# Five small tables moved between the large on-chip buffers of a two-model transformer kernel

## Chip, core and metric

One core of a Trainium2 chip runs the whole program in one launch. The metric is the time of one execution on the device in microseconds (us). Its engines are TensorE (PE: matmuls; its weight loads are listed apart as PEld), VectorE (DVE), ScalarE (ACT), GpSimd (POOL) and SyncE (SP, which here only issues transfers).

## What is computed

256 tokens of width 1024 pass through two blocks, each of two layers, all in float32. Cut to its large products:

```python
for l in range(2):                                   # first block
    mod = silu(c) @ ada_w[l] + ada_b[l]              # nine shifts, scales and gates
    hn = modulate(rms_norm(h)); h = h + 0.5*g1 * ((silu(hn @ gate) * (hn @ up)) @ w_out)     # ffn1, width 2816
    hn = modulate(rms_norm(h)); z = hn @ w_in[l]     # 2564 columns: diff attention, conv, gMLP, forgetting attention
    h = h + g2 * (mixed @ w_out[l])
    hn = modulate(rms_norm(h)); h = h + 0.5*g3 * swiglu(hn)                                  # ffn2, width 2816
for l in range(2):                                   # second block
    proj = rmsnorm(x) @ w_in_2[l]                    # 7680 columns: q, k, v of 24 heads, and gates
    x = x + (gates * three attention outputs) @ w_o
    x = x + square(relu(rmsnorm(x) @ w_up)) @ w_down # width 4096
```

## The kernel before

**Weights in parts.** The large products aren't done in plain float32. Each float32 weight chunk is split into a rounded high part and a rest: SP loads 1 MB chunks (128 partitions x 8 k-tiles x 256 columns) into the four slots of `ring`; ACT writes the high part (`round_half`, L1187: `w_hi <- ring`); POOL writes the low part (`split`, L682: `w_lo = ring - w_hi`), both in halves of a chunk, and `w_hi` and `w_lo` have two slots each. The activations are split too: `hn`/`hn_lo` hold the normed input (8 k-tiles x 256 tokens), and the hidden layers lie in `gated` and `up2`, two views of the one large buffer `arena`. A product of a k-tile and 128 output columns is then three matmuls of 256 moving columns in fp32r, issued by `terms` (L716 in the trace):

```python
for i, (a, b) in enumerate(((w, x), (w, x_lo), (w_lo, x))):
    if token_major:
        a, b = b, a
    last = mm(out, a, b, start=start and i == 0, stop=stop and i == 2)
```

The first of `a, b` is the stationary operand, which a weight load (PEld) brings in, 128 columns of 4 bytes (512 bytes a partition); the second streams, 256 columns of 4 bytes (1024 bytes a partition). A weight chunk of 8 k-tiles and 256 columns is 8 x 2 x 3 = 48 matmuls. `product` reads `hn` and `hn_lo` (phases f1in, z, f2in, z2, up) and `out_product` reads `gated` or `up2` (f1out, f2out, dn). In v-type units of z and z2 (`token_major`) hn and hn_lo are the stationary operands and the weights' parts stream. The first unit of a phase, whose k-tiles come in one after another, has lines of its own (L747, L748, L751). The products `o`, `y` and `wo` (L800, L1124) are plain float32 straight from `ring` with moving operands in `arena`.

**Order of the work.** Each engine's program is written out by hand and synchronised by counting semaphores. `fill` on SP waits until POOL is done with the ring slot. While f1in and f2in run, SP also loads 2 MB chunks of `ada_w` into `arena` (`ada_fill`), one after every pair of weight chunks, for DVE to reduce (L1558). Attention heads (L929, L963, L964, L707) are interleaved with units of z2 in the second block.

**Where buffers begin.** The buffers in a partition are laid one behind the other in the order of their declarations; each begins at a multiple of 32 bytes. A slice that a matmul reads begins a multiple of 512 bytes behind its buffer's start, for `w_hi`, `w_lo`, `hn`, `hn_lo`, `gated` and `up2` alike, so the distance of two operands modulo 512 bytes is that of their buffers. Before, all from `w_hi` to `const` have sizes that are multiples of 512 bytes and so begin at distance 0; `const` has 3959 columns, and behind it come `mod` (288 bytes), `der` (256), `cond` (32), `norm2` (160), `stat` (256), `small` (256), `ident_r` and `unseen` (512 each), then `arena`.

Of the kernel before, what the change touches and what calls it, by code (L numbers as in the profile page):

```python
# [19 lines left out]
F32R = mybir.dt.float32r  # L20
# [6 lines left out]
S = 256  # L27
L = 2
KT = D // P
# [5 lines left out]
MOD_TILES = 9 * KT  # L35
# [353 lines left out]
def build(nc, dram, out, at, old):  # L389

    plan = Plan()
    with ExitStack() as ctx:
        def sb(name, *shape, dtype=F32):
            return ctx.enter_context(nc.sbuf_tensor(name, [P, *shape], dtype))
# [5 lines left out]
        ring = sb("ring", RING, 8, 256)  # L400
        w_hi, w_lo = sb("w_hi", 2, 8, 256, dtype=F32R), sb("w_lo", 2, 8, 256, dtype=F32R)
        h = sb("h", KT, S)
        hn, hn_lo = sb("hn", KT, S, dtype=F32R), sb("hn_lo", KT, S, dtype=F32R)
        square, square_sum = sb("square", 2, S), sb("square_sum", S)
        rstd = sb("rstd", S)
        n_const = dram["constants"].shape[1]
        const = sb("const", n_const)
        mod = sb("mod", MOD_TILES)
        der = sb("der", 64)
        cond = sb("cond", KT)  # L410
        norm2 = sb("norm2", 40)
        stat = sb("stat", 4, 16)
        small = sb("small", 64)
        ident_r, unseen = sb("ident_r", P, dtype=F32R), sb("unseen", P, dtype=F32R)
        arena = sb("arena", ARENA)
        arena_at = nc.sbuf_base - 4 * ARENA

# [1644 lines left out]
```

## Time and profile before

| | |
|---|---|
| median of 3 runs | 2059.44 us (2059.37 to 2059.82) |
| the profiled execution's own time | 2062.2 us |
| its span | 2060.4 us, 36118 instructions |
| mean granted TensorE clock | 0.981 of full speed |
| PE busy | 1981.9 us (96%), 15210 matmuls |
| PEld busy | 1905.0 us (92%) |
| POOL busy | 1320.9 us (64%) |
| ACT busy, DVE busy | 939.7 us (46%), 826.5 us (40%) |
| moved by DMA | 398.21 MB, mean 193 GB/s |

The span runs from the first to the last instruction; the own time of an execution is 1.8 us more. Matmuls are pipelined, so that a record's length (its mean ns) is longer than the distance from its start to the next one's; how fast PE goes is seen by counting matmuls in a stretch. Idle time of an engine that nobody waits for costs nothing.

### The profile page before, as it was taken

What the parts mean: (1) busy time and instruction counts of PE and PEld (TensorE: products, weight loads), DVE (VectorE), ACT (ScalarE), POOL (GpSimd) and SP (SyncE); (2) the same over time, 40 slices, a digit from 0 to 9 for tenths busy, and PEclk for the clock granted to TensorE, in tenths of its full rate; (3) what the DMA queues carried; (4) which work ended last, traced back from release to release, by engine and by line L of the source; (5) the groups of instructions that cost most, each with busy time, mean ns of one, the idle gap of its engine ahead of it and who ended that gap; (6) DMA issues with size and microseconds to landing.
All of it is one profiled execution on the core that took longest, in us unless ns stands there. A gap on an engine that the chain in (4) does not pass through costs nothing.

```text
span 2060.4 us, 36118 instructions
## 1 busy us (share of the span) xinstructions
PE 1981.9 (96%) x15210; PEld 1905.0 (92%) x15210; DVE 826.5 (40%) x1747; ACT 939.7 (46%) x1467; POOL 1320.9 (64%) x612
## 2 busy tenths in 40 slices
PE   6999997999999999889999999999999999999998
PEld 3999996899999998779999999989999999989998
DVE  3674576372147466735113522133302522133311
ACT  2444554344454445434445354534544354525543
POOL 0888760388878887217887865506897955506895
PEclk8999998999999999999999999999999999999999
DMA  9998650695599786127545643346564643335562
GB/s 319 361 341 294 215 158 21 212 360 167 182 306 364 267 261 190 65 80 259 190 159 174 203 143 113 114 128 193 184 200 136 222 144 103 123 123 185 184 205 82
DMA packets 356786, 398.21 MB, mean 193 GB/s; under 512 B 8984, under 2 KB 318992, under 8 KB 356624
## 3 DMA queue, kind: packets, MB, share of 16 engines
q1 hardware_dynamic: 356464, 395.70, 58.5%
q8 instruction: 120, 1.97, 0.4%
q14 instruction: 42, 0.34, 0.1%
q10 hardware_dynamic: 160, 0.20, 0.0%
HBM read 394.82 MB, written 1.05 MB: 192 GB/s over the span
## 4 chain that ended last, share of the span: by engine, by line
PE 88%; DVE 4%; ACT 3%; POOL 1%; issue 1%; SPq 1%; DMA 1%; DVEq 0%; ACTq 0%
PE bank L716 70%; PE bank L800 6%; PE bank L1124 3%; POOL w_lo L682 1%; PE bank L963 1%; PE bank L929 1%; SPq L544 1%; DVE arena L1701 1%; DVE bank L1630 1%; ACT arena L1323 1%; PE bank L707 1%; PE bank L751 1%; PE bank L747 1%; ACT w_hi L1187 1%; PE bank L1025 1%
## 5 line engine op out<-in xcount | busy, mean ns | idle before, releaser
L682 POOL TENSOR_TENSOR w_lo<-ring,w_hi 128x1024 fp32r<-128x1024 f32 (+2 forms) x608 | 1320.7, 2198 | 720.0 <-ACT w_hi L1187 719.8
L716 PE MATMUL bank<-hn,w_hi 128*128 128x256 f32 x2752 | 786.3, 286 | 3.3 <-POOL w_lo L682 2.9
L716 PE MATMUL bank<-hn_lo,w_hi 128*128 128x256 f32 x2752 | 778.6, 283 | 0.0
L716 PE MATMUL bank<-hn,w_lo 128*128 128x256 f32 x2752 | 778.6, 283 | 0.0
L1187 ACT ACTIVATE w_hi<-ring 128x1024 fp32r<-128x1024 f32 (+2 forms) x608 | 578.6, 976 | 416.2 <-PE bank L716 381.1
L716 PEld LDWEIGHTS bank<-hn,w_hi 128*128 128x128 f32 x2752 | 527.9, 192 | 7.1 <-POOL w_lo L682 5.3
L716 PEld LDWEIGHTS bank<-hn_lo,w_hi 128*128 128x128 f32 x2752 | 528.0, 192 | 1.1 <-issue 0.5
L716 PEld LDWEIGHTS bank<-hn,w_lo 128*128 128x128 f32 x2752 | 527.9, 192 | 0.0
L716 PE MATMUL bank<-gated,w_hi 128*128 128x256 f32 x1408 | 239.6, 276 | 0.0
L716 PEld LDWEIGHTS bank<-gated,w_hi 128*128 128x128 f32 x1408 | 212.0, 188 | 0.0
L716 PE MATMUL bank<-gated,w_lo 128*128 128x256 f32 x704 | 194.3, 276 | 0.0
L716 PE MATMUL bank<-up,w_hi 128*128 128x256 f32 x1024 | 174.2, 276 | 0.0
L1558 DVE SCALAR_TENSOR_TENSOR bank<-arena,cond,bank 128x512 f32<-128x512 f32 x204 | 154.2, 756 | 7.3
L716 PEld LDWEIGHTS bank<-up,w_hi 128*128 128x128 f32 x1024 | 154.1, 188 | 0.0
L716 PE MATMUL bank<-up,w_lo 128*128 128x256 f32 x512 | 141.3, 276 | 0.0
L716 PEld LDWEIGHTS bank<-gated,w_lo 128*128 128x128 f32 x704 | 132.1, 188 | 0.0
L800 PE MATMUL bank<-arena,ring 128*128 128x256 f32 x512 | 116.1, 390 | 5.1 <-DVE arena L1994 3.2
L800 PEld LDWEIGHTS bank<-arena,ring 128*128 128x128 f32 x512 | 100.1, 196 | 20.7 <-DVE arena L1994 4.0
L1658 DVE TENSOR_TENSOR bank<-arena,bank 128x512 f32<-128x512 f32 x44 | 30.6, 696 | 219.5 <-PE bank L716 219.5
L1275 ACT ACTIVATE arena<-bank 128x512 f32<-128x512 f32 x44 | 26.3, 598 | 172.8 <-PE bank L716 172.2
L1323 ACT ACTIVATE arena<-arena,stat 128x128 f32<-128x128 f32 x120 | 53.2, 444 | 102.7 <-DVE stat L1715 44.0
L716 PEld LDWEIGHTS bank<-up,w_lo 128*128 128x128 f32 x512 | 96.1, 188 | 0.0
(203 smaller groups left out, 2222.4 us busy)
## 6 DMA issues: line engine op xcount, KB each, us to landing
ring<-in_ffn_w_in SPq DMA_DIRECT2D x88, 1024.0 KB, 6.7
ring<-in_w_in SPq DMA_DIRECT2D x72, 1024.0 KB, 5.1
arena<-in_ada_w SPq DMA_DIRECT2D x35, 2048.0 KB, 10.2
ring<-in_w_up SPq DMA_DIRECT2D x32, 1024.0 KB, 5.5
ring<-in_w_down SPq DMA_DIRECT2D x32, 1024.0 KB, 5.1
ring<-in_ffn_w_out SPq DMA_DIRECT2D x32, 768.0 KB, 4.7
ring<-in_ffn_w_out SPq DMA_DIRECT2D x32, 640.0 KB, 4.1
ring<-in_w_in SPq DMA_DIRECT2D x16, 512.0 KB, 3.7
```

The costliest lines, as they stand in the source:

```text
L544: sp.dma_start(dst, src).then_inc(rows_in, 16)
L682: pool.tensor_tensor(w_lo[:, q, ks], ring[:, r, k0:k0 + n], w_hi[:, q, ks], ALU.subtract) \
L707: i = pe.transpose(dst, src, ident[0:n, 0:n])
L716: last = mm(out, a, b, start=start and i == 0, stop=stop and i == 2)
L747: mm(outs[c], w_hi[:, q, kw, ws], hn[:, kx], start=kx == 0 and c == 0, stop=False)
L800: last = mm(outs[c], ring[:, s, k, c * P:(c + 1) * P], x[:, k0 + k, :], start=(k0 + k == 0), stop=(k0 + k == total - 1))
L1124: last = mm(b[:, c], ring[:, s, k0 + k, c * P:(c + 1) * P], o2[:, k0 + k, :], start=(k == 0), stop=(k == nk - 1))
L1187: f(w_hi[:, q, half * 4:half * 4 + n], ring[:, r, k0:k0 + n], ACT.Copy).then_inc(weights_rounded, 1)
L1275: f(act_tmp[:, j], bank[:, 2 * j], ACT.Silu).then_inc(silu_done, eng.step(f"{s} silu {p}", silu_done))
L1323: f(t, t, ACT.Exp, bias=st[:, b + j:b + j + 1], scale=scale, accum_out=st[:, 10 + 2 * m + j:11 + 2 * m + j]) \
L1558: stt(part, src[:, k], col(cond, k), part, ALU.mult, ALU.add).then_inc(vector_done, eng.step())
L1658: tt(bank[:, 2 * j], act_tmp[:, j], bank[:, 2 * j + 1], ALU.mult) \
```

## The change

Only declarations move. `der` is laid before `hn`; `mod`, `cond` and a new unused `spare` of 16 columns lie between `hn` and `hn_lo`; a new unused `more` of 24 columns lies before `arena`. No instruction is added, removed or put elsewhere in any engine's order, and all sizes, slices and waits stay; line numbers behind the place grow by one (L716 becomes L717).

```diff
         h = sb("h", KT, S)
-        hn, hn_lo = sb("hn", KT, S, dtype=F32R), sb("hn_lo", KT, S, dtype=F32R)
+        der = sb("der", 64)
+        hn = sb("hn", KT, S, dtype=F32R)
+        mod, cond, spare = sb("mod", MOD_TILES), sb("cond", KT), sb("spare", 16)
+        hn_lo = sb("hn_lo", KT, S, dtype=F32R)
         square, square_sum = sb("square", 2, S), sb("square_sum", S)
         rstd = sb("rstd", S)
         n_const = dram["constants"].shape[1]
         const = sb("const", n_const)
-        mod = sb("mod", MOD_TILES)
-        der = sb("der", 64)
-        cond = sb("cond", KT)
         norm2 = sb("norm2", 40)
         stat = sb("stat", 4, 16)
         small = sb("small", 64)
         ident_r, unseen = sb("ident_r", P, dtype=F32R), sb("unseen", P, dtype=F32R)
+        more = sb("more", 24)
         arena = sb("arena", ARENA)
```

Added up, the buffers begin at these distances from `w_hi`, modulo 512 bytes:

| buffer | before | after |
|---|---|---|
| ring, w_lo, h | 0 | 0 |
| hn | 0 | 256 |
| hn_lo | 0 | 128 |
| square, square_sum, rstd, const | 0 | 128 |
| arena (so gated, up2 and the attention's views) | 192 | 352 |

Distances within `arena` stay as they were, and so does the distance of `ring` to the weights' parts.

## Rows read from the trace of the kernel before

**Rows 1.** The page: span, busy time, and the chain that ended last, by line

```profile
span 2060.4 us, 36118 instructions
PE 1981.9 (96%) x15210; PEld 1905.0 (92%) x15210; DVE 826.5 (40%) x1747; ACT 939.7 (46%) x1467; POOL 1320.9 (64%) x612
PE 88%; DVE 4%; ACT 3%; POOL 1%; issue 1%; SPq 1%; DMA 1%; DVEq 0%; ACTq 0%
```

**Rows 2.** PE's groups by form: count, busy us, mean ns, idle before and its releaser

```profile
L716 PE MATMUL bank<-hn,w_hi 128*128 128x256 f32 x2752 | 786.3, 286 | 3.3 <-POOL w_lo L682 2.9
L716 PE MATMUL bank<-hn_lo,w_hi 128*128 128x256 f32 x2752 | 778.6, 283 | 0.0
L716 PE MATMUL bank<-hn,w_lo 128*128 128x256 f32 x2752 | 778.6, 283 | 0.0
L716 PE MATMUL bank<-gated,w_hi 128*128 128x256 f32 x1408 | 239.6, 276 | 0.0
L716 PE MATMUL bank<-gated,w_lo 128*128 128x256 f32 x704 | 194.3, 276 | 0.0
L716 PE MATMUL bank<-up,w_hi 128*128 128x256 f32 x1024 | 174.2, 276 | 0.0
L716 PE MATMUL bank<-up,w_lo 128*128 128x256 f32 x512 | 141.3, 276 | 0.0
...
L716 PE MATMUL bank<-w_lo,hn 128*128 128x256 f32 x288 | 81.4, 283 | 0.0
...
L747 PE MATMUL bank<-hn,w_hi 128*128 128x256 f32 x160 | 46.5, 309 | 15.3 <-ACT hn L1247 11.0 <-ACT hn L1245 4.2
```

**Rows 3.** The chain in 950:1000, products of hn: start us, us, matmuls

```profile
949.95 50.16 PE bank L716 x418
```

**Rows 4.** The chain in 1500:1550, products of up2

```profile
1500.00 50.09 PE bank L716 x442
```

**Rows 5.** Windows of 50 us: PE, PEld, DVE, ACT, POOL, clock, DMA share, GB/s

```profile
950.00:1000.00 50.00, 50.00 (x419) 50.00 (x418) 14.41 (x21) 21.93 (x26) 41.94 (x18) 1.00 0.54 172
1500.00:1550.00 50.00, 50.00 (x443) 50.00 (x443) 2.99 (x7) 20.68 (x23) 46.42 (x20) 1.00 0.61 197
1900.00:1950.00 50.00, 50.00 (x419) 50.00 (x419) 17.56 (x26) 24.95 (x35) 42.02 (x18) 1.00 0.61 190
```

**Rows 6.** Timeline of PE from 269.75, token-major units: start us, us

```profile
269.75 0.28 PE L716 MATMUL bank<-w_hi,hn 128*128 128x256 f32 x1
269.87 0.28 PE L716 MATMUL bank<-w_hi,hn_lo 128*128 128x256 f32 x1
269.99 0.28 PE L716 MATMUL bank<-w_lo,hn 128*128 128x256 f32 x1
```

**Rows 7.** PE in 1346:1371, plain float32 with ring and arena

```profile
L1124 PE MATMUL bank<-arena,ring 128*128 128x256 f32 x117 | 25.4, 379 | 0.0
```

**Rows 8.** POOL's groups by form, whole span

```profile
L682 POOL TENSOR_TENSOR w_lo<-ring,w_hi 128x1024 fp32r<-128x1024 f32 x448 | 1064.3, 2401 | 646.3 <-ACT w_hi L1187 646.1
```

**Rows 9.** Windows over the stages that also load ada_w, columns as in Rows 5

```profile
60.00:160.00 100.00, 100.00 (x836) 100.00 (x835) 71.50 (x98) 43.13 (x51) 83.88 (x36) 1.00 1.06 350
...
600.00:670.00 70.00, 70.00 (x585) 70.00 (x585) 52.89 (x73) 31.47 (x38) 57.91 (x26) 1.00 1.06 360
```

**Rows 10.** Timeline of ACT from 148.98, idle before and its releaser in brackets

```profile
149.48 2.00 ACT L1187 ACTIVATE w_hi<-ring 128x1024 fp32r<-128x1024 f32 x2
151.97 1.06 ACT L1187 ACTIVATE w_hi<-ring 128x1024 fp32r<-128x1024 f32 x1 [0.50 <-DMA ring<-in_ffn_w_in]
```

**Rows 11.** The chain in the second block's attention, from 1208.62

```profile
1208.62 0.67 PE bank L929 x4
1209.46 0.29 DVE arena L1701
...
1211.07 2.44 DVE arena L1745 x6
...
1214.82 1.54 ACT arena L1323 x7
1216.57 0.68 ACT arena L1323 x3
1217.25 3.79 ACT w_hi L1187 x4
...
1251.76 5.76 PE bank L716 x48
```

## The prediction

> **What bounds the kernel now.** I read the page first. PE is busy for 96% of the span and the chain that ended last is PE for 88% of it [rows 1]; what makes matmuls quicker is worth its full size, and little else is. The groups by form come next, because they keep operands apart [rows 2]. All fp32r products have the same shape, 128x128 stationary and 256 moving columns, and yet the records of those with hn and hn_lo last 283 to 286 ns, and those with gated and up (the view up2) 276 ns. Records overlap, so this doesn't give the rate. The rate is read from the chain in a stretch with nothing but such matmuls: 418 matmuls with hn in 50.16 us, 120.0 ns each [rows 3], against 442 with up in 50.09 us, 113.3 ns each [rows 4]. In both stretches PE and PEld are busy throughout and the granted clock is 1.00 (2.4 GHz) [rows 5]: no wait and no clock accounts for the 6.7 ns.
>
> Is it what the other engines do meanwhile? The windows say no [rows 5]: with DVE busy 14.41 us of 50 or 17.56 us, the count with hn is 419 both times; in the faster stretch POOL is busier (46.42 us against 41.94), and so is the DMA (197 GB/s against 172). The token-major units, where hn is the stationary operand and w_hi and w_lo stream, start every 0.12 us as well [rows 6]. So it lies in the pair of buffers, whichever side streams. Two things set the pairs apart: hn and hn_lo begin 0 bytes from w_hi and w_lo modulo 512, gated and up2 192 bytes; and hn lies near the weights' parts (within some 57 KB) while arena lies far off. The change alters the first and hardly the second.
>
> **The change, part by part.** No instruction is added, removed or moved, so the sum has only rates in it.
>
> *hn 0 to 256 bytes, hn_lo 0 to 128.* L716 has 3 x 2752 matmuls on them [rows 2] and 3 x 288 more in token-major form (one of its three rows stands there): 9120. L747, L748 and L751 add 3 x 160 = 480 [rows 2], which I leave out: they wait for the norm's k-tiles (15.3 us before L747) and run partly at the lower clock. No row shows distances of 256 and 128. The bounds: from above, 120.0 ns as now (nothing excludes a loss, but no fp32r row is slower at full clock); from below, the quickest streaming that the trace shows. Plain float32 takes 25.4 us for 117 records of 256 columns [rows 7], 217 ns each. As 256 columns at 2.4 GHz, one a cycle, are 106.7 ns, I count such a record as two passes, and half of it, 108.5 ns, is my estimate for a stream that meets no hindrance. I take 113.3 ns, the only measured value of the same instruction at a distance other than 0: 9120 x 6.67 ns = 60.8 us.
>
> *arena 192 to 352 bytes.* 2112 matmuls with gated and 1536 with up [rows 2], 3648 in all. Now 113.3 ns; bounds again 108.5 and 120.0 ns, thus -17.5 us to +24.4 us. Both distances are off 0, so I take no change.
>
> *const, square, mod, der, cond.* Their matmuls are few and their ACT and DVE work has 50% and more idle time; nothing.
>
> *What is not passed on.* Three covers get thinner. (a) POOL: a chunk costs it 2 x 2.40 us = 4.80 us [rows 8] and PE 48 x 0.1200 = 5.76 us now, 5.44 us at 113.3 ns, 5.21 us at 108.5 ns. PE stays the slower one; 0. (b) The ring's loads while ada_w is loaded too: a pair of chunks and one ada chunk are 4 x 1.049 MB = 4.19 MB. In 11.52 us that is 364 GB/s, in 10.88 us 385 GB/s; the windows show 350 to 360 GB/s at a DMA share of 1.06 [rows 9], which is full. In the first f1in the ring already loses its lead: at 151.97 ACT waits 0.50 us for the ring's transfer [rows 10]. There some 16 chunks x 48 x 6.67 ns = 5.1 us of PE's gain runs into the data's arrival; ACT and POOL work about half a chunk ahead of PE, which takes back some 2 us, so 3 us are lost. In the later ones (600:670) ACT doesn't wait for a transfer, and I take nothing off. (c) In the second block's attention some stretches have DVE and ACT on the chain [rows 11], about 25 us a layer, with some 5 chunks of matmuls beside it: 2 x 5 x 48 x 6.67 ns = 3.2 us lost; where heads and 48-matmul units alternate on the chain (1251.76) the gain counts fully.
>
> Sum: 60.8 - 3 - 3.2 = 54.6 us. The profiled execution's own 2062.2 us becomes 2007.6 us; the runs shown have a median 2.8 us lower, so I forecast 2059.4 - 54.6 = 2004.8, say 2005 us.
>
> **A rule against it.** The rows show two rates for one instruction, 120.0 and 113.3 ns [rows 3, 4]. The Trainium skill, "SBUF — State Buffer", section "Who interferes with whom", gives PE two independent read ports, one for the moving operand and one for the weight load, and says that PE waits for nobody; by that the distance between the two operands can't matter, and the sum would be 0. It offers no reason for the 6.7 ns that the rows show, so I weigh it as what speaks for the no-change rival and not as the likeliest. Its page "TensorE: Matmul & The Clock Gate", section "Back-to-back issue gap", has 2.5 ns above the columns' time for a warm matmul, 109.2 ns here; every fp32r row of this trace is above it, and by it the sum for the whole would be 9120 x 10.8 + 3648 x 4.1 = 113 us, before covers.
>
> **The rivals.**
> - *Deeper gain.* 120.0 ns is 13.3 ns above the 106.7 ns in which 256 columns pass at 2.4 GHz, and 113.3 ns is 6.7 ns above: exactly half. If the weight load and the stream meet at some addresses, 192 bytes may be halfway and 128, 256 or 352 free. For it: room down to 108.5 ns. Against: no fp32r pair shows it. At the bound: 9120 x 11.5 + 17.5 us = 122 us, less some 8 us for (b) and (c), so 1945 us; with hn halfway to it, 1980 us.
> - *Only a part.* The repeating length may be 256 bytes, not 512: then hn at 256 is as bad as at 0, and only what pairs with hn_lo gets better, a third: 3040 x 6.67 = 20 us, 2039 us. For it: 192 and 0 differ modulo 256 as well.
> - *No change.* What matters is near or far (the same part of the memory), not the distance modulo 512. For it: each hn pair is near and each arena pair far, so the trace can't tell; the skill's two ports lean this way. Against: regular 120.0 ns for hn and hn_lo, w_hi and w_lo, though they lie at different distances in bytes. 2059 us.
> - *Slower.* Arena's new distance falls where the old one of hn was, while hn gains nothing: 3648 x 6.67 = +24 us, 2084 us; f1out, f2out and dn would be the places. It decides when hn gains less than 0.4 of what arena loses per matmul (3648/9120), i.e. under 2.7 ns against 6.7 ns.
>
> **How the numbers follow.** Forecast 0.46, deeper 0.22, a part 0.12, no change 0.12, slower 0.08. A measurement of this kernel can tell 0.2% (4 us) from nothing. Faster: 0.46 + 0.22 + 0.12 = 0.80; same 0.12; slower 0.08. The range has to keep 8 in 10: it takes in the first three, from 1945 us to 2045 us (20 us saved, and some of it lost). The likeliest case by itself is 1983 to 2020 us: 111 ns (9120 x 9.0 = 82 us) to 115 ns (9120 x 5.0 = 46 us), less the 6.2 us of covers.
>
> **What would show it.** The chain or count in a stretch of hn matmuls: 441 in 50 us instead of 418, records about 276 ns instead of 283. In stretches with up and gated still 441 to 443; any other count is arena's distance. If hn's three kinds get different spacings, the length that repeats is shorter than 512. The first f1in should show ACT waiting several us for ring<-in_ffn_w_in, against 0.5 us at 151.97. POOL's share in hn stretches should rise to about 44 us of 50. Wrong would be: 120 ns for hn still (then it is the region), or POOL's subtraction taking longer at the new addresses, since it has only 0.64 us a chunk to spare at 113.3 ns. All of it is read in stages, not in the sum: plain float32 (L1124, L800) should stay at 217 ns.

## The result, and the profile after

The changed kernel takes 2065.49 us (median of 16 runs) against 2060.28 us for the kernel before (16 runs): ratio 1.0023, 95% interval 1.0016 to 1.0030. It is 0.2% slower, where 2.6% faster (2005 us) was forecast, and it lies above the forecast range, which ended at 2045 us. The page of its profiled execution:

```profile
span 2064.3 us, 36118 instructions
PE 1985.2 (96%) x15210; PEld 1911.1 (93%) x15210; DVE 826.9 (40%) x1747; ACT 940.4 (46%) x1467; POOL 1319.5 (64%) x612
PE 88%; DVE 4%; ACT 3%; POOL 1%; issue 1%; SPq 1%; DMA 1%; DVEq 0%
L717 PE MATMUL bank<-hn,w_hi 128*128 128x256 f32 x2752 | 777.9, 283 | 2.1 <-POOL w_lo L683 1.8
L717 PE MATMUL bank<-hn,w_lo 128*128 128x256 f32 x2752 | 769.7, 280 | 0.0
L717 PE MATMUL bank<-gated,w_hi 128*128 128x256 f32 x1408 | 253.6, 283 | 0.0
L717 PE MATMUL bank<-up,w_hi 128*128 128x256 f32 x1024 | 184.4, 282 | 0.0
```

The page's totals hardly differ from those of before [rows 1]: same share of PE, same chain. The groups do differ, and in two directions: hn's records got a little shorter (283 and 280 ns for 286 and 283), those of gated and up longer (283 and 282 for 276) [rows 2]. The rates are in the chain of the same two stretches, 950:1000 for hn and 1500:1550 for up:

```profile
949.99 50.06 PE bank L717 x425
```

```profile
1500.00 50.04 PE bank L717 x417
```

With hn 50.06 us / 425 = 117.8 ns (it was 120.0 [rows 3]); with up 50.04 / 417 = 120.0 ns (it was 113.3 [rows 4]). The 864 token-major matmuls on hn gained less; in a stretch of them, 1648:1660, the chain has 119.2 ns each:

```profile
1647.93 12.16 PE bank L717 x102
```

Added up, 8256 x -2.2 ns and 864 x -0.8 ns are -19 us, and 3648 x +6.7 ns are +24 us, together +5 us. The medians differ by 5.2 us, the two profiled spans by 2064.3 - 2060.4 = 3.9 us. The change did act, by some 20 us on each side, and the sum hides it.

Nothing else moved by as much. POOL's subtraction takes what it took [rows 8], and in the first f1in ACT waits for the ring's transfer a little more than before (1.23 us where it was 0.50 [rows 10]); the rows of POOL by form and of ACT's timeline after:

```profile
L683 POOL TENSOR_TENSOR w_lo<-ring,w_hi 128x1024 fp32r<-128x1024 f32 x448 | 1062.2, 2396 | 638.6 <-ACT w_hi L1188 637.8
```

```profile
151.65 1.06 ACT L1188 ACTIVATE w_hi<-ring 128x1024 fp32r<-128x1024 f32 x1 [1.23 <-DMA ring<-in_ffn_w_in]
```

### The profile page after: what moved, and what is told of

The parts are those of the page before. It is cut to its first block, busy times and chain, and to the rows that moved or that the text cites. A ratio compares the mean times of both kernels' runs of the same rounds, so it can differ in the third digit from the quotient of the medians.

```text
span 2064.3 us, 36118 instructions
## 1 busy us (share of the span) xinstructions
PE 1985.2 (96%) x15210; PEld 1911.1 (93%) x15210; DVE 826.9 (40%) x1747; ACT 940.4 (46%) x1467; POOL 1319.5 (64%) x612
## 4 chain that ended last, share of the span: by engine, by line
PE 88%; DVE 4%; ACT 3%; POOL 1%; issue 1%; SPq 1%; DMA 1%; DVEq 0%
PE bank L717 71%; PE bank L801 6%; PE bank L1125 3%; POOL w_lo L683 1%; PE bank L964 1%; PE bank L930 1%; DVE arena L1702 1%; SPq L545 1%; DVE bank L1631 1%; ACT arena L1324 1%; PE bank L748 1%; PE bank L708 1%; ACT w_hi L1188 1%; PE bank L752 1%; PE bank L1026 1%
## 5 line engine op out<-in xcount | busy, mean ns | idle before, releaser
L717 PE MATMUL bank<-hn,w_hi 128*128 128x256 f32 x2752 | 777.9, 283 | 2.1 <-POOL w_lo L683 1.8
L717 PE MATMUL bank<-hn_lo,w_hi 128*128 128x256 f32 x2752 | 775.1, 282 | 0.0
L717 PE MATMUL bank<-hn,w_lo 128*128 128x256 f32 x2752 | 769.7, 280 | 0.0
L717 PEld LDWEIGHTS bank<-hn,w_hi 128*128 128x128 f32 x2752 | 517.8, 188 | 5.9 <-POOL w_lo L683 3.9
L717 PEld LDWEIGHTS bank<-hn,w_lo 128*128 128x128 f32 x2752 | 519.3, 189 | 0.0
L717 PEld LDWEIGHTS bank<-hn_lo,w_hi 128*128 128x128 f32 x2752 | 516.7, 188 | 1.0 <-issue 0.5
L717 PE MATMUL bank<-gated,w_hi 128*128 128x256 f32 x1408 | 253.6, 283 | 0.0
L717 PEld LDWEIGHTS bank<-gated,w_hi 128*128 128x128 f32 x1408 | 215.8, 187 | 0.0
L717 PE MATMUL bank<-gated,w_lo 128*128 128x256 f32 x704 | 197.3, 280 | 0.0
L717 PE MATMUL bank<-up,w_hi 128*128 128x256 f32 x1024 | 184.4, 282 | 0.0
L717 PEld LDWEIGHTS bank<-up,w_hi 128*128 128x128 f32 x1024 | 157.7, 188 | 0.0
L717 PE MATMUL bank<-up,w_lo 128*128 128x256 f32 x512 | 144.2, 282 | 0.0
L717 PEld LDWEIGHTS bank<-gated,w_lo 128*128 128x128 f32 x704 | 133.9, 190 | 0.0
L717 PEld LDWEIGHTS bank<-up,w_lo 128*128 128x128 f32 x512 | 96.6, 189 | 0.0
```

## Experiments

### A map of distances (e1_map)

The kernel's stages give one distance each. This program measures many: it fills one fp32r buffer from x and runs 46 streams of 96 matmuls with nothing else going on, each stream on a source line of its own. The distances go up in steps of 32 bytes, so that each stream stands behind the one with the next smaller distance.

```python
for a in run(0, 41152, 8192, 0): last = mm(a[0], a[1], a[2], start=a[3], stop=a[4])  # near 192
```

The arguments are where w_hi and x begin (bytes), how far behind x its low part is, and whether it is token-major.

> A measuring program, not the model: it fills one large fp32r buffer and then runs 46 streams of 96 matmuls with the shapes, slices and order of the products (w_hi,x; w_hi,x_lo; w_lo,x; eight k-tiles, two column halves, twice), one stream a source line, with x at a set distance from the weights, near (40960 bytes and the distance) or far (112128 bytes and the distance). Its output is not the model's. Distance theory: the time per matmul is a function of the distance of weights and x modulo 512 bytes alone. Then near and far give the same at each of the 16 distances, with 120.0 ns at 0, 113.3 ns at 192, 119.9 ns at 352, 117.8 ns for 256 with the low part at 128, and moving both operands by 64 bytes changes nothing. Place theory: what counts is whether the two operands lie near or far, or their own addresses. Then near stays at 118 to 120 ns at every distance and far 0 is at 113 ns, or moving both by 64 bytes changes the time.

The timeline of the map, start us and us of each stream, for near 0 (L78), near 192 (L84), near 256 (L86), far 0 (L94) and their followers:

```profile
62.86 11.68 PE L78 MATMUL bank<-buf 128*128 128x256 f32 x96
74.37 11.48 PE L79 MATMUL bank<-buf 128*128 128x256 f32 x96
...
131.16 11.07 PE L84 MATMUL bank<-buf 128*128 128x256 f32 x96
142.07 11.52 PE L85 MATMUL bank<-buf 128*128 128x256 f32 x96
153.43 11.68 PE L86 MATMUL bank<-buf 128*128 128x256 f32 x96
164.94 11.47 PE L87 MATMUL bank<-buf 128*128 128x256 f32 x96
...
243.99 11.68 PE L94 MATMUL bank<-buf 128*128 128x256 f32 x96
255.50 11.48 PE L95 MATMUL bank<-buf 128*128 128x256 f32 x96
...
312.29 11.07 PE L100 MATMUL bank<-buf 128*128 128x256 f32 x96
323.20 11.52 PE L101 MATMUL bank<-buf 128*128 128x256 f32 x96
```

A start taken from the next one and divided by 96 is the time per matmul: (74.37 - 62.86) / 96 = 119.9 ns at 0, (142.07 - 131.16) / 96 = 113.6 ns at 192, (164.94 - 153.43) / 96 = 119.9 ns at 256. (A stream's first few matmuls are still off its steady rate; in its second half 192 is at 113.3.) In the same way for all, from the starts before they are rounded to 10 ns, in ns. "Near" has the moving buffer 40960 bytes and the distance behind the weights, "far" 112128 bytes and the distance; the rows "+ 256" have the distances 256 to 480:

```
distance          0      32     64     96     128    160    192    224
near            119.9  117.8  117.8  119.8  118.7  117.3  113.7  118.3
near, + 256     119.9  117.8  117.8  119.8  118.7  117.3  113.7  118.3
far             119.9  117.8  117.8  119.8  118.7  117.3  113.7  118.3
far, + 256      119.9  117.8  117.8  119.8  118.7  117.3  113.7  118.3

both moved by 64: 119.9 at 0, 113.5 at 192, 119.8 at 256, 120.0 at 352
hi at 256, lo at 128: 116.8 near, 116.7 far
token-major: 119.9 at 0, 113.3 at 192, 120.0 at 256, 117.3 at 352
at 4, 8, 16, 48 bytes: 123.2, 117.7, 116.7, 118.3
```

The place theory is out: near and far agree at every distance, and moving both operands by 64 bytes changes nothing beyond 0.2 ns. The distance counts, but it repeats after 256 bytes, not 512. Among the multiples of 32 bytes, 192 (and 448) is the one good value in this map, by 3.6 ns to the next. Arena had it before, by accident; the change took it to 352, which is 96, as bad as 0. And hn went from 0 to 256, which is 0.

Two rows don't fit the distance as the only cause. In token-major form 352 has 117.3 ns and not 120.0, so at some distances it also matters which operand streams. And 256 with the low part at 128 was expected at 117.8 ns, as in the changed kernel, but has 116.7 to 116.8 ns here. The changed kernel itself has both rates: 117.8 ns in 950:1000 above, and 7.93 us / 68 = 116.6 ns in 280:288, a stretch of the same plain hn products:

```profile
280.15 7.93 PE bank L717 x68
```

So already this pair of distances has more than one rate.

### The change in two halves (e2_arena352, e3_hn256_128)

```diff
+        more = sb("more", 40)
         arena = sb("arena", ARENA)
```

> Kernel before with 40 unused columns laid before arena, so that only arena moves, from 192 to 352 bytes; hn and hn_lo stay at 0. Distance theory: products with gated and up go from 113.3 to 120 ns, 3648 x 6.7 ns = 24 us more, 2084 us (1.2% slower); products with hn stay at 120.0 ns. Rival, that the changed kernel's arena products are slow because of something else that moved with the tables: they stay at 113.3 ns and the time at 2060 us.

Measured 2086.24 us against 2061.67 us, ratio 1.0120 (1.0103 to 1.0137): +24.6 us. The chain in 1500:1550 of this kernel (up), then in 950:1000 (hn):

```profile
1499.98 50.04 PE bank L717 x417
```

```profile
949.99 50.04 PE bank L717 x417
```

Both are 120.0 ns: up pays the full 6.7 ns and hn stays where it was.

The other half, from the changed kernel:

```diff
-        small = sb("small", 64)
+        small = sb("small", 48)
...
-        more = sb("more", 24)
         arena = sb("arena", ARENA)
```

> Changed kernel with arena back at 192 (the unused 24 columns before it left out, and small cut from 64 to 48 columns, of which 44 are used), so that hn stays at 256 and hn_lo at 128. Distance theory: products with hn at 117.8 ns, those with gated and up at 113.3 ns: 9120 x 2.2 ns = 20 us less than before, 2040 us (1.0% faster). Rival, that moving hn made arena's products slower: those at about 120 ns and the time near 2064 us.

Measured 2042.70 us against 2061.67 us, ratio 0.9909 (0.9894 to 0.9923): -19.0 us. Chain in 950:1000 (hn) and 1500:1550 (up):

```profile
949.93 50.17 PE bank L716 x426
```

```profile
1499.96 50.09 PE bank L716 x442
```

These are 117.8 ns and 113.3 ns. The halves add up: +24.6 - 19.0 = +5.6 us, against the 5.2 us between the two medians. One thing did not fit: the second layer's up, in 1940:1990, counts 427 in 50 us (PE, by window), 117 to 118 ns, where the first layer's has 113.3 at the same distances.

```profile
1940.00:1990.00 50.00, 50.00 (x427) 1.00 0.62 197
```

The buffers are the same in both layers, so the distance alone doesn't account for it; the next kernel shows the same more clearly.

### All at 192 (e4_all192)

```diff
+        cond, norm2 = sb("cond", KT), sb("norm2", 40)
         hn, hn_lo = sb("hn", KT, S, dtype=F32R), sb("hn_lo", KT, S, dtype=F32R)
...
-        cond = sb("cond", KT)
-        norm2 = sb("norm2", 40)
```

> Kernel before with cond and norm2 (32 and 160 bytes) laid before hn instead of before stat: hn, hn_lo and arena all at 192 bytes from the weights' parts. Distance theory: every fp32r product at 113.3 ns, 9120 x 6.7 = 61 us less on hn, of which some 6 us are lost where the ring's loads and attention bound: 2005 us (2.7% faster). Place theory: hn lies near and doesn't reach 113.3 ns, at best the 117.8 ns of the changed kernel: 2040 to 2060 us.

Measured 2031.20 us against 2061.67 us, ratio 0.9854 (0.9840 to 0.9869): a gain of 30.5 us, about half of what the distance theory gave, and more than the place theory allowed. Three windows of this kernel (us; PE busy and count; clock; DMA share; GB/s), two of hn and one of gated:

```profile
430.00:480.00 50.00, 50.00 (x444) 1.00 0.86 287
600.00:650.00 50.00, 50.00 (x427) 1.00 1.07 367
520.00:560.00 40.00, 40.00 (x342) 1.00 0.57 180
```

444 in 50 us is 113.3 ns, 427 is 117.8 ns, the same instructions on the same buffers; gated in 520:560, which had 113.3 ns before, is at 117.8 ns too. Where does it turn? In the chain of 440:490 and behind it:

```profile
439.90 48.28 PE bank L715 x426
488.18 0.80 PE bank L836 x8
```

```profile
489.90 20.14 PE bank L715 x171
```

Up to 488.18 it is 48.28 / 426 = 113.3 ns; then stand eight records of the sum over ada_w's columns (L836, 24 columns each); behind them it is 20.14 / 171 = 117.8 ns, and it stays so to the end of the phase and through all of gated.

### What stands ahead (e5_map_entry, e6_states)

> The measuring program again (its output is not the model's), near place only, at 37 distances from 0 to 248 bytes in steps of 8 and some of 4; each distance twice with 96 matmuls: once behind a stream at distance 0, once behind eight small plain float32 matmuls of 32 columns, as the sums of ada_w stand ahead of the out products in the kernel. Entry theory: at one distance the stream can settle at more than one rate, and what stands ahead of it picks which; at 192 it is 113.3 ns behind the distance-0 stream and 117.8 ns behind the small matmuls, which is how the kernel with all at 192 has both. Rival, that the other engines' traffic does it: here only TensorE works, so both entries give 113.3 ns at 192. Beside that the finer steps tell whether any distance gives under 113 ns for both entries.

At 192 the rival seemed right: behind the distance-0 stream 192 has 113.6 ns, and behind the eight small matmuls 113.5 ns (114.3 with the first start, which takes 201 ns, in the mean). No 117.8 appeared, so at 192 this one way of entry told nothing on the kernel's. At other distances it did: TensorE alone settled at two rates at 80 (120.0 and 118.3 ns), 136 (122.2 and 120.0 ns) and 180 (123.3 and 120.0 ns), the first behind a stream at 0, the second behind the small matmuls. The timeline at 136 (L151 behind the stream, L153 behind the small ones):

```profile
688.41 11.89 PE L151 MATMUL bank<-buf 128*128 128x256 f32 x96
700.15 1.87 PE L79 MATMUL bank<-src 128*128 128x32 f32 x16
701.85 11.77 PE L153 MATMUL bank<-buf 128*128 128x256 f32 x96
713.46 11.67 PE L154 MATMUL bank<-buf 128*128 128x256 f32 x96
```

L151 takes (700.15 - 688.41) / 96 = 122.3 ns, L153 takes (713.46 - 701.85) / 96 = 120.9 ns with its slow first start and 120.0 ns without. Nor does the distance of the stream just ahead settle it: at 32 bytes this run has 116.7 ns and the map 117.8 ns, both behind a stream at 0. So what stands ahead counts at many distances, and the table above holds for one order of streams.

The finer steps also found a second good distance, 112, with 113.3 ns once settled, and nothing below 113.3. Values close to 192 are bad (180: 123.3, 188: 118.6, 196: 121.7, 200: 120.0, all behind a stream at 0).

> The measuring program a third time (its output is not the model's). At distances 192 and 112 a stream of 96 matmuls is interrupted by 1 to 4 small plain float32 matmuls of 8 to 128 columns and goes on with 96 more; then six pairs of distances for the high and the low part, each entered in four ways. Phase theory: the stream's rate depends on where the weight load stands against the stream when it starts, so some of the 24 interruptions turn 113.3 ns at 192 into 117.8 ns, which stays until the next interruption; a continued stream never changes by itself. Rival, other engines' traffic: with TensorE alone all 24 give 113.3 ns.

The interruption is one line between two streams. Its arguments are the columns of each small matmul, their count, and the column at which their stationary operand begins. Columns and count are varied; the place goes with the count (0 for one and four, 32 for two, 96 for three):

```python
for a in run(0, 41152, 8192, 0): last = mm(a[0], a[1], a[2], start=a[3], stop=a[4])  # 192 ahead
small(8, 2, 32)
for a in run(0, 41152, 8192, 0): last = mm(a[0], a[1], a[2], start=a[3], stop=a[4])  # 192 behind 2 small of 8
```

The timeline at 192, with one small matmul (two records of L79), with two, with three, and with four:

```profile
73.72 0.28 PE L79 MATMUL bank<-src 128*128 128x8 f32 x2
73.86 11.13 PE L84 MATMUL bank<-buf 128*128 128x256 f32 x96
84.83 11.04 PE L85 MATMUL bank<-buf 128*128 128x256 f32 x96
95.71 0.51 PE L79 MATMUL bank<-src 128*128 128x8 f32 x4
96.07 11.55 PE L87 MATMUL bank<-buf 128*128 128x256 f32 x96
107.46 11.47 PE L88 MATMUL bank<-buf 128*128 128x256 f32 x96
118.77 0.73 PE L79 MATMUL bank<-src 128*128 128x8 f32 x6
119.35 11.55 PE L90 MATMUL bank<-buf 128*128 128x256 f32 x96
...
142.05 0.95 PE L79 MATMUL bank<-src 128*128 128x8 f32 x8
142.86 11.14 PE L93 MATMUL bank<-buf 128*128 128x256 f32 x96
153.83 11.04 PE L94 MATMUL bank<-buf 128*128 128x256 f32 x96
```

L85 takes (95.71 - 84.83) / 96 = 113.3 ns; behind two small matmuls L87 and the whole of L88 take (118.77 - 107.46) / 96 = 117.8 ns; behind four it is back at 113.3. Of 24 interruptions at 192, ten give 117.8 ns (two and three small ones of 8, 16, 24, 64 and 128 columns), and none of the streams that simply go on changes. So at 192 there are two steady rates, and what stands ahead picks one. TensorE was alone here: the other engines aren't needed for it. Whether the count or the place picks the rate isn't shown, since they were changed together: all twelve interruptions from column 0 end fast, and ten of the twelve from column 32 or 96, both 128 bytes modulo 256, end slow.

At 112, all 24 interruptions end at 113.3 ns, some after a few slower matmuls. The timeline there, with four small ones of 16 columns:

```profile
774.23 0.96 PE L79 MATMUL bank<-src 128*128 128x16 f32 x8
775.04 11.17 PE L177 MATMUL bank<-buf 128*128 128x256 f32 x96
786.05 11.04 PE L178 MATMUL bank<-buf 128*128 128x256 f32 x96
```

Mixed pairs (one part at 192, the other at 0, 64 or 112, either way round) were all between 115.5 and 119.3 ns once the first start's 85/96 = 0.9 ns is taken off, that of 192 and 112 included. None of these six reaches the 113.3 ns of both parts at the same good distance.

### A kernel on 112 (e7_all112, e8_hn192_arena112)

A buffer begins at a multiple of 32 bytes, and 112 is not one, so the rest comes from unused columns inside the buffer:

```diff
-        hn, hn_lo = sb("hn", KT, S, dtype=F32R), sb("hn_lo", KT, S, dtype=F32R)
+        both = sb("hn", 28 + 2 * KT * S, dtype=F32R)
+        hn, hn_lo = (both[:, 28 + i * KT * S:28 + (i + 1) * KT * S].rearrange("p (k s) -> p k s", k=KT) for i in range(2))
...
+        more = sb("more", 8)
         arena = sb("arena", ARENA)
...
-        gated = rounded("gated", 8192, FT, 2, S)
+        gated = rounded("gated", 8192, 4 + FT * 2 * S)[:, 4:].rearrange("p (f a s) -> p f a s", f=FT, a=2)
...
-        up2 = rounded("up2", 0, 32, 2, S)
+        up2 = rounded("up2", 0, 4 + 32 * 2 * S)[:, 4:].rearrange("p (f a s) -> p f a s", f=32, a=2)
```

> Kernel before with every fp32r operand pair at 112 bytes modulo 256: hn and hn_lo in one buffer behind 28 unused columns, gated and up2 behind 4 unused columns of their views and arena 96 bytes modulo 256. Period theory with one steady rate at 112: 8256 products of hn at 113.3 ns from whatever stands ahead, gated and up at 113.3 ns as before, the 864 token-major ones at 118.7 ns (distance -112 = 144): 55 + 1 us less, of which 6 us are not passed on: 2011 us (2.4% faster). Rival, that the kernel's other traffic spoils the rate as well: parts of the hn stages stay at 117 to 118 ns as in the kernel with all at 192, about 2030 us.

Measured 2013.79 us against 2061.11 us, ratio 0.9775 (0.9758 to 0.9792): -47.3 us, where -50 was expected. The same three windows as for the kernel with all at 192:

```profile
430.00:480.00 50.00, 50.00 (x443) 1.00 0.85 283
600.00:650.00 50.00, 50.00 (x444) 1.00 1.07 365
520.00:560.00 40.00, 40.00 (x355) 1.00 0.64 204
```

It is 113.3 ns in all three windows: hn in 600:650 has 444 for 427 at the same DMA share, gated 355 for 342 beside a higher one. The rival falls. One part of the expectation failed: the token-major matmuls, expected at 118.7 ns, run at 14.52 / 121 = 120.0 ns, as before.

```profile
1605.99 14.52 PE bank L718 x121
```

In this form 112 isn't a good distance, though 192 had 113.3 ns in the map. PE also waits longer for POOL's low parts than the 2.9 us of before [rows 2], and ACT 31.7 us in all for the ring's transfers of ffn_w_in, 23.6 us before:

```profile
PE bank L718 <- POOL w_lo L684: 6.0, 9, 1.3
```

The numbers are the us in all, how many times, and the longest one.

The last one has hn at 192 (cond and norm2 ahead of it, as above), gated and up2 as in this one, and 40 unused columns ahead of arena.

> The kernel with all at 192, but gated and up2 at 112 bytes modulo 256. hn then still has two rates. Period theory: gated no longer takes over the slow rate that hn's stream leaves (2112 x 4.5 ns = 9.5 us), so 2031 - 9.5 = 2022 us (1.9% faster than before), with gated and up at 113.3 ns everywhere. Rival: gated stays at 117.8 ns and the time at 2031 us.

Measured 2019.39 us against 2061.11 us, ratio 0.9799 (0.9783 to 0.9815), -41.7 us where -39 was expected. Its chain in 525:545 (gated) and its window 620:690 (hn):

```profile
524.97 20.06 PE bank L716 x177
```

```profile
620.00:690.00 70.00, 70.00 (x597) 1.00 0.94 318
```

Gated is at 20.06 / 177 = 113.3 ns, where it took over the slow rate in the kernel with all at 192; hn in 620:690 still has the slow rate (70 us / 597 = 117.3 ns). The fastest version by its median is thus all at 112, 2.3% under the kernel before and 2.5% under the changed one; its interval and that of the kernel with hn at 192 overlap a little.

## Why the prediction was wrong, point by point

- **What bounds the kernel** held: a few ns per matmul are worth their full size. In the two halves +24.6 us came of 24.4 computed beforehand and -19.0 of 20.
- **That it lies in the pair of buffers, and in their distance** held: TensorE alone shows rates of the same size, near and far alike. The Trainium skill, "SBUF — State Buffer", section "Who interferes with whom", gives PE two independent read ports and lets it wait for nobody. By that the distance couldn't matter and the sum would be 0, and these runs disagree: the distance of the two operands moves a matmul by up to 9.7 ns (113.6 against 123.3). "Whichever side streams" holds at 0 and 192 in the map, but not at 352 (120.0 ns one way, 117.3 the other), nor at 112 in the kernel (113.3 ns one way, 120.0 the other).
- **"I take 113.3 ns, the only measured value of the same instruction at a distance other than 0"** is the step that failed. It made one value at 192 stand for every distance but 0. Measured for 256 with the low part at 128: 117.8 ns for the plain products and 119.2 ns for the token-major ones, so about 19 us instead of 60.8. Two rows, one at 0 and one at 192, can't give a function of the distance; the upper bound of 120.0 ns stood there and should have weighed as much as the middle.
- **"Both distances are off 0, so I take no change"** failed by the same thought, with the other sign: 352 is 96 modulo 256 and costs 120.0 ns, +24.4 us, the upper bound that was named. What was missed is that a change that moves a good distance risks something; the only measured good one was 192, and it was given up.
- **The rivals.** "Slower" had arena's part almost exactly, and hn gained 2.2 ns, under the 2.7 ns from which it was to decide; that this case had 0.08 is the error of the chances. "Only a part" had the length of 256 right; that its 20 us for hn came out as well is luck. It took 120.0 ns for two thirds of the matmuls and 113.3 ns for those with hn_lo at 128, but 128 by itself has 118.7 ns in the map, and the mixed pair has rates of its own, 117.8 and 116.7 ns; its 2039 us also kept arena's products at 113.3 ns. "Deeper gain" found nothing: no distance tried is under 113.3 ns.
- **The covers** were hardly touched by the change itself, which gained too little. In the kernel with all at 112, 8256 x 6.7 = 55 us would come off the plain hn products; 47.3 us were measured, about 8 us lost, where 6.2 were taken. Part of it fits cover (b), the ring's loads: PE waits some 3 us more for POOL's low parts. Another part is the slower matmuls after each interruption. How the loss divides isn't shown, and (c) wasn't measured apart.
- **A rival that was not there**: more than one rate at one distance. It took much of the gain of the kernel with all at 192. No row of before shows it: there hn is at 0, which had 120.0 ns behind either entry, and gated and up have 113.3 ns.
- **The 109.2 ns** of the prediction's rule, and its 113 us, were not reached: no stream of fp32r matmuls here went under 113.3 ns.

## What to carry to other kernels

Where fp32r matmuls follow each other with a weight load each, count them by operand pair in stretches without waits; a few ns between pairs of one shape point at where their buffers begin, not at the engines. Before buffers are moved for it, measure all distances in one small program, in both forms if both are used, and each with several things standing ahead of it, since one distance may have more than one rate. When an interruption is varied, vary one thing of it at a time. An accidental distance may be the best one: write down which it is before tables are added or removed, because 160 bytes ahead of a large buffer cost 1.2% here.

## What was not expected of the hardware

- The time of a weight load and an fp32r matmul of 256 columns depends on the distance of the two operands modulo 256 bytes: 113.3 ns at 112 and 192 with the weights' parts stationary, 116 to 121 ns at most others, and up to 121.5 to 123.3 ns at 4, 72, 136, 180 and 196 behind another stream.
- What stands ahead can pick between rates of one distance. At 192 they are 113.3 and 117.8 ns and hold for hundreds of matmuls (426 and 171 in one piece) until something else comes between; at 136 they are 122.2 and 120.0 ns. At 112 every one of 24 interruptions came back to 113.3 ns.
- Why 256 bytes, what picks the rate, and why 113.3 ns is the least are open. A meeting of the weight load and the stream at the same part of the memory is a guess; no run looks into a matmul.
